# Key and query chunks of a hybrid decoder layer: one 512-column product over a whole bank in place of two of 256 columns

## What is computed

```
u = rms_norm(h, mix_norm_g)
proj = u @ w_in
q, k, v, z, xbc, dt_raw, qm, gate_logits = jnp.split(proj, split_points, axis=-1)
...
s_own = jnp.einsum('bhqd,bhjd->bhqj', q_c, k_own) + bias_tab[:, t5_bucket(dist_own)]
p_own = softmax(where(dist_own >= 0, s_own, -inf))
o = jnp.einsum('bhqj,bhjd->bhqd', p_own, v_own)
```

## Time and profile before

| | |
|---|---|
| time, median of 3 runs | 683.9 us (683.73 to 683.92) |
| span of the profiled execution | 682.1 us |
| TensorE busy | 674.4 us, 99% of the span |
| VectorE busy | 493.9 us, 72% |
| ScalarE busy | 370.9 us, 54% |
| mean granted TensorE clock | 0.998 |

### The profile page before, as it was taken

One profiled execution on the slowest core, in us unless ns is written; L12 is line 12 of the kernel. 1 busy time (PEld: TensorE's weight loads), 2 busy tenths in 40 slices (PEclk: granted clock), 3 DMA queues, 4 the chain that ended last, 5 costly groups with the idle time before them and its releaser, 6 DMA issues.

```text
span 682.1 us, 11413 instructions
## 1 busy us (share of the span) xinstructions
PE 674.4 (99%) x4505; PEld 616.7 (90%) x4505; DVE 493.9 (72%) x618; ACT 370.9 (54%) x461; POOL 10.6 (2%) x21
## 2 busy tenths in 40 slices
PE   9999999999999999999999999999999999999996
PEld 6999999999999989999888888888899999999995
DVE  6886979696866766777754655556688777777796
ACT  6568867767455544555533333443555555555552
POOL 0000000000100100000000000000100000000001
PEclk9999999999999999999999999999999999999999
DMA  9775768569185457545566665565445555555521
GB/s 298 239 255 180 247 206 257 165 217 326 62 260 181 144 165 232 177 144 182 165 213 218 215 191 184 193 227 178 168 136 194 187 185 185 188 187 185 192 88 62
DMA packets 99599, 130.92 MB, mean 192 GB/s; under 512 B 5615, under 2 KB 73708, under 8 KB 98924
## 3 DMA queue, kind: packets, MB, share of 16 engines
q1 hardware_dynamic: 98020, 125.27, 56.5%
q10 hardware_dynamic: 1544, 5.16, 2.4%
HBM read 129.31 MB, written 2.68 MB: 193 GB/s over the span
## 4 chain that ended last, share of the span: by engine, by line
PE 98%; DVE 1%; ACT 0%; issue 0%; POOL 0%; POOLq 0%; DVEq 0%
PE ps L364 30%; PE ps L365 30%; PE ps L366 30%; PE ps L676 1%; PE ps L413 1%; PE ps L419 1%; PE ps L661 1%; PE ps L677 1%; PE ps L696 1%; PE ps L713 1%; PE ps L704 0%; DVE h_nat L1744 0%; PE ps L695 0%; PE ps L715 0%; PE ps L769 0%; PE ps L664 0%
## 5 line engine op out<-in xcount | busy, mean ns | idle before, releaser
L336 DVE TENSOR_TENSOR w_lo<-w_raw,w_hi 128x2048 fp32r<-128x2048 f32 x107 | 244.6, 2287 | 88.1 <-ACT w_hi L332 88.1
L332 ACT ACTIVATE w_hi<-w_raw 128x2048 fp32r<-128x2048 f32 x107 | 204.3, 1911 | 100.0 <-PE ps L366 93.9
L364 PE MATMUL ps<-tok_hi,w_hi 128*128 128x256 f32 x864 | 246.6, 285 | 0.4 <-DVE tok_lo L1305 0.4
L365 PE MATMUL ps<-tok_lo,w_hi 128*128 128x256 f32 x864 | 244.4, 283 | 0.0
L366 PE MATMUL ps<-tok_hi,w_lo 128*128 128x256 f32 x864 | 244.4, 283 | 0.0
L364 PEld LDWEIGHTS ps<-tok_hi,w_hi 128*128 128x128 f32 x864 | 165.7, 192 | 2.0 <-DVE w_lo L1299 0.8
L365 PEld LDWEIGHTS ps<-tok_lo,w_hi 128*128 128x128 f32 x864 | 165.7, 192 | 0.4
L366 PEld LDWEIGHTS ps<-tok_hi,w_lo 128*128 128x128 f32 x864 | 165.7, 192 | 0.0
L364 PE MATMUL ps<-w_hi,tok_hi 128*128 128x512 f32 x128 | 50.2, 392 | 0.0
L365 PE MATMUL ps<-w_lo,tok_hi 128*128 128x512 f32 x128 | 49.9, 390 | 0.0
L366 PE MATMUL ps<-w_hi,tok_lo 128*128 128x512 f32 x128 | 49.8, 389 | 0.0
(11 more groups left out here) (268 smaller groups left out, 1003.5 us busy)
## 6 DMA issues: line engine op xcount, KB each, us to landing
w_raw<-w_in SPq DMA_DIRECT2D x94, 512.0 KB, 4.8
w_raw<-w_ffn_up SPq DMA_DIRECT2D x44, 512.0 KB, 4.4
w_raw<-w_ffn_down SPq DMA_DIRECT2D x22, 512.0 KB, 4.1
w_raw<-w_mem_kv SPq DMA_DIRECT2D x16, 512.0 KB, 4.6
w_raw<-w_br_ssm SPq DMA_DIRECT2D x16, 512.0 KB, 4.9
acs_b<-acs_d ACTq DMA_DIRECT2D x4, 1024.0 KB, 6.6
w_raw<-w_br_attn SPq DMA_DIRECT2D x8, 512.0 KB, 4.9
w_raw<-w_br_mem SPq DMA_DIRECT2D x8, 512.0 KB, 4.5
```

What stands on the lines that cost most here:

```text
L332: act.activation(w_hi[:, s, :], w_raw[:, s, :], ACT.Copy).then_inc(hi_ready[s], 1)
L336: dve.tensor_tensor(w_lo[:, s, :], w_raw[:, s, :], w_hi[:, s, :].bitcast(F32), ALU.subtract).then_inc(lo_ready[s], 1)
L364: pe.matmul(o, a[0], b[0], start=start, stop=False, **kw)
L365: pe.matmul(o, a[0], b[1], start=False, stop=False, **kw)
```

## The change

`tok_hi` and `tok_lo` are laid beside each other, so that the 512 columns of both parts are one moving operand. For the key and query chunks `gemm_both` takes the place of `gemm_cols`: the weights' high part times both token parts in one product of 512 columns over a whole bank, then the weights' low part times the tokens' high part, 256 columns, onto the first half. Each half `j` now has a bank of its own: banks 0 and 1 for keys, 3 and 4 for the queries of pair 0, 6 and 7 for those of the other pairs. The second half of each bank has to be added to the first: ScalarE copies the second halves into `k_t` (a new instruction) or `q_t`, and VectorE adds the first halves (in place of its key copy, and new for the query). Since bank 7 also holds the attention output of pair 0 and of pair 1, the second half of a query chunk waits for `oa_lo_s`. Two semaphores of the memory norm become one, and no transfer is moved.

```diff
+K_BANKS = (0, 1)
...
-    tok_hi = place("tok_hi", 72, [KT, T], F32R)
-    tok_lo = place("tok_lo", 80, [KT, T], F32R)
+    tok = place("tok", 72, [KT, 2, T], F32R)
+    tok_hi, tok_lo = tok[:, :, 0, :], tok[:, :, 1, :]
...
+    def gemm_both(pe, r, s, banks, both, other=None):
+        pe.wait_ge(lo_ready[s], r + 2)
+        pe.wait_ge(bank_free[s], r + 1)
+        for j in range(2):
+            if other is not None and j:
+                pe.wait_ge(*other)
+            for k in range(KT):
+                w = slice(k * CW + j * P, k * CW + (j + 1) * P)
+                pe.matmul(ps[:, banks[j], :], w_hi[:, s, w], both[:, k], start=k == 0, stop=False)
+                mm = pe.matmul(ps[:, banks[j], 0:T], w_lo[:, s, w], both[:, k, 0, :], start=False, stop=k == KT - 1)
+        mm.then_inc(gemm_done[s], 1)
...
+    def q_banks(i):
+        return (6, 7) if i else (3, 4)
+    def part_pair(banks, n):
+        return ps[:, banks[0]:banks[1] + 1, n * T:(n + 1) * T]
...
-            gemm_cols(pe, RB, 0, tok_hi, tok_lo)
-            gemm_cols(pe, RB, 1, tok_hi, tok_lo)
+            pe.wait_ge(xdt_ready, NT * GROUPS)
+            pe.wait_ge(bank_free[1], RB + 1)
+            gemm_both(pe, RB, 0, K_BANKS, tok)
+            gemm_both(pe, RB, 1, q_banks(0), tok)
...
             for i in range(1, 4):
-                gemm_cols(pe, RB + i, 0, tok_hi, tok_lo)
+                if i == 1:
+                    pe.wait_ge(y_step, GT * GROUPS)
+                gemm_both(pe, RB + i, 0, K_BANKS, tok)
                 if i > 1:
                     pe.wait_ge(oa_lo_s, i - 2)
                     pe.wait_ge(group_var, 1)
                     attend(i - 1)
                 turn_probs(i)
-                gemm_cols(pe, RB + i, 1, tok_hi, tok_lo)
+                gemm_both(pe, RB + i, 1, q_banks(i), tok, (oa_lo_s, i - 1))
                 gemm_wide(pe, RB + i, i % 2, tok_hi, tok_lo)
                 if i == 1:
+                    pe.wait_ge(bank_free[1], RB + 3)
                     group_sums()
                 scores(i)
...
+                act.wait_ge(gemm_done[0], r + 1)
+                act.activation(k_t[:], part_pair(K_BANKS, 1), ACT.Copy).then_inc(low_part, 1)
                 split_hi(act, r + 1, 0)
...
                 act.wait_ge(gemm_done[1], r + 1)
-                act.activation(q_t[:], halves(1), ACT.Copy, scale=DH ** -0.5).then_inc(bank_free[1], 1)
+                act.activation(q_t[:], part_pair(q_banks(i), 1), ACT.Copy, scale=DH ** -0.5).then_inc(low_part, 1)
...
-                dve.wait_ge(gemm_done[0], r + 1)
-                dve.tensor_copy(k_t[:], halves(0)).then_inc(bank_free[0], 1)
+                dve.wait_ge(low_part, 2 * i + 1)
+                dve.tensor_tensor(k_t[:], part_pair(K_BANKS, 0), k_t[:], ALU.add).then_inc(bank_free[0], 1)
                 split_lo(dve, r + 1, 0)
...
+                dve.wait_ge(low_part, 2 * i + 2)
+                dve.scalar_tensor_tensor(q_t[:], part_pair(q_banks(i), 0), DH ** -0.5, q_t[:], ALU.mult,
+                                         ALU.add).then_inc(bank_free[1], 1)
                 split_lo(dve, r + 1, 1)
```

More of the change, by code:

```diff
@@ L269, in build @@
         sem, ("group_mm", "group_var", "group_pow", "group_kept", "rstd_g_in"))
+    low_part = sem("low_part")
     s_mm, s_biased, s_max, s_neg, p_exp, p_rec, p_norm, p_turned, pt_ready, o_mm, oa_hi_s, oa_lo_s = map(
@@ L274, in build @@
     norm_step, os_hi_s, os_lo_s = map(sem, ("norm_step", "os_hi_s", "os_lo_s"))
-    m_in, m_sumsq, m_var, m_rstd, m_scaled, mx_in, m_factor_kept, m_factor_in, m_hi, m_lo = map(
-        sem, ("m_in", "m_sumsq", "m_var", "m_rstd", "m_scaled", "mx_in", "m_factor_kept", "m_factor_in", "m_hi", "m_lo"))
+    m_in, m_sumsq, m_var, m_rstd, m_scaled, mx_in, m_factor_moved, m_hi, m_lo = map(
+        sem, ("m_in", "m_sumsq", "m_var", "m_rstd", "m_scaled", "mx_in", "m_factor_moved", "m_hi", "m_lo"))
     ms_mm, ms_max, ms_neg, mp_exp, mp_rec, mp_norm, mp_turned, mo_mm, om_hi_s, om_lo_s = map(
@@ L1105, in _ @@
             act.wait_ge(m_rstd, NT)
-            act.dma_start(m_factor_d.rearrange("(p t) -> p t", p=P), stat[:, 2:2 + NT]).then_inc(m_factor_kept, 16)
+            act.dma_start(m_factor_d.rearrange("(p t) -> p t", p=P), stat[:, 2:2 + NT]).then_inc(m_factor_moved, 16)
             def mem_high(j):
@@ L1112, in _ @@
             squares(GROUPS)
-            act.wait_ge(m_factor_kept, 16)
-            act.dma_start(m_factor[:], on_all(m_factor_d, T)).then_inc(m_factor_in, 16)
+            act.wait_ge(m_factor_moved, 16)
+            act.dma_start(m_factor[:], on_all(m_factor_d, T)).then_inc(m_factor_moved, 16)
             for i in range(1, 4):
@@ L1511, in heads @@
                 if i == 1:
-                    dve.wait_ge(m_factor_in, 16)
+                    dve.wait_ge(m_factor_moved, 32)
                     dve.wait_ge(mx_in, 16)
```

## The result

The changed kernel takes 696.81 us (median of 5 runs, 693.94 to 698.72) against 683.92 us (5 runs, 683.73 to 684.80): 1.0183 times as long, interval 1.017 to 1.0196. It is 12.9 us slower; the forecast was 10.5 us slower.

What follows compares the result with a forecast made beforehand. TensorE's own stream was taken as the bound, since it hardly waits. -1.5 (products) + 6.5 and 3.3 (waits) + 2.2 (clock) = +10.5 us, from 683.9 to 694.4 us; own range 692.4 to 695.8, 8-in-10 range 691.0 to 697.4.

Steps and rivals of the forecast that it cites:

- the second rival: TensorE's clock falls in both `oa_lo` waits: 2.2 us more than the forecast, 696.6 us, chance 0.21.
- products: Key and query chunks: 348 ns a block instead of 360, over 128 blocks, 1.5 us gained; bounds 0 and 2.5.
- wait in pair 2: Pair 2's query chunk: TensorE stands for `oa_lo` from 218.6 to 225.1, 6.5 us; bounds 6.0 and 6.9.
- wait in pair 3: Pair 3's query chunk: TensorE stands for `oa_lo` of the pair 2 scores' softmax, 3.3 us; bounds 2.9 and 3.8.
- other new waits: `xdt_ready`, `y_step`, the query's release by VectorE, pair 0's earlier transposes: price 0, at most 0.2 us.
- clock behind the first wait: TensorE's clock falls to its lower level in pair 2's wait: 2.2 us lost; bounds 0 and 2.7.
- clock behind the second wait: Pair 3's 3.3 us wait: loss from a fall of TensorE's clock taken as 0; bounds 0 to 2.7 us.
- The clock of that working: Times for pair 2's wait, counted from the key chunk's start at 208.07 us; the whole stretch moves earlier by earlier gains.
- The 0.48 us taken for ScalarE's key copy: Pair 2: the new copy delays the high part as the like-shaped query copy delayed its next instruction, 222.41 to 222.89.
- I take 0 for it: Pair 3's 3.3 us wait, barely as long as the idle time before the end's clock fall: no clock loss.
- The change of shape costs nothing there: Feed-forward stage: where a 512 follows a 256 the starts lie 0.12 us apart, 613.65 to 613.77.
- the prediction's own line of 0.35 us a block: Key and query chunks: the prediction is wrong if alternating products step wider than 0.35 us a block.

Runs made afterwards that it cites:

- without waits: Changed kernel with high and low parts of the attention output of pairs 0 and 1 moved earlier, new products kept: 683.05 us, 0.9989 times before.
- first wait filled: Changed kernel with 26 products on zeros put ahead of the wait for `oa_lo` in pair 2's query chunk: 694.32 us, ratio 1.0151.
- the second move alone: Changed kernel with only pair 1's `oa_lo` moved earlier, so the wait in pair 2 stays: 691.53 us, ratio 1.0113.
- both waits filled: Changed kernel with 26 products on zeros in pair 2's wait and 11 more in pair 3's: 692.82 us, ratio 1.0129.
- the first move alone: Changed kernel with only pair 0's `oa_lo` moved earlier, so the short wait in pair 3 stays: 687.87 us, ratio 1.0065.
- the grouped order: Kernel with both `oa_lo` moved, each half chunk's 8 products of 512 columns first, its 8 of 256 behind: 682.62 us, ratio 0.9985.

## Why the prediction was right, and what it mis-sized

The range held the time and the side was right. The forecast's case was that the clock falls in one wait; by the runs it falls in both, which was the second rival (696.6 us, chance 0.21). The range of 691.0 to 697.4 us held the 696.81 because it took that rival in: the forecast's own range ended at 695.8. Nor does that own range follow from its bounds. With 0 to 2.7 us for the clock at each wait they give 691.3 to 698.5. That the rival came within 0.2 us is partly luck, since its two falls were priced 0.4 us too high together and its gain 0.6 us too large. In order of the prediction's terms:

| term | forecast, us | measured, us | from |
|---|---|---|---|
| products | -1.5 | -0.9 | without waits against before, medians |
| wait in pair 2 | +6.5 | +6.4 | waits (6.5 as a step between starts) |
| wait in pair 3 | +3.3 | +3.1 | waits (3.2 as a step) |
| other new waits | 0 | 0 | no row names them |
| clock behind the first wait | +2.2 | +2.5 | change against first wait filled (2.1 by the second move alone) |
| clock behind the second wait | 0 | +1.5 | first against both waits filled (1.7 by the first move alone) |
| sum | +10.5 | +12.6 | 12.9 by the medians |

**The waits.** Place, cause and length were as worked out. The clock of that working ran 0.70 us late as a whole, as it had said it might: the query chunk began at 215.00, not 215.70, and `oa_lo` ended at 224.37, not 225.1. Both moved alike, so their difference stood. The 0.48 us taken for ScalarE's key copy from its like was 0.47.

**The clock.** The step that failed is "I take 0 for it" for the second wait. It rested on one row, the fall some 3 us behind the program's last product, and took a wait of 3.3 us for too close to that to count. In the profiled execution of the change this held, as the clock stayed full behind 3.07 us of standing. Where only this wait was left, and where the first was filled, profiles show it fallen behind 3.07 and 3.12 us. Taking 0 for an event on the edge was the wrong reduction: worked as a coin's toss it would have added about 0.9 us (half of 1.7). The first wait's 2.2 was inside its bounds, 0.3 below the 2.5 that the medians give; the profiled execution itself lost only 1.39 there. The 2.2 was sized by the program's start, where products on zeros ran some 5.5 us at half pace. Behind the waits less was lost in each of the four falls that were profiled, 1.4 to 1.7 us. The start is also a row read by pace alone, as the granted clock in that trace stands at 1.00 from 0 to 8 us. What decides in which execution a wait of 3 us makes the clock fall is open. That the five runs of the change spread over 4.8 us, and those with the first or both waits filled over 0.2, fits a loss behind the first wait that varies with where the wait ends. This is argued from the spread and not shown, since only one execution of each kernel was profiled, and the kernel with the short wait alone spread over 1.6 us too.

**The products.** Both spacings were right for products of one shape, and the term was too large: 0.9 us by the medians and 0.98 by the chunks of the traces, where 1.5 was forecast. "The change of shape costs nothing there" was read off a single change from 256 to 512. In the change, six blocks from 215.43 to 217.56 take 355 ns each, not 348, while six from 243.36 to 245.44 take 347. The wider step crosses the prediction's own line of 0.35 us a block, beyond which it called itself wrong. So the gain differs by chunk: pair 3's key chunk went from 5.93 to 5.84 us and pair 2's from 5.93 to 5.74, where 0.19 was forecast for each. Of the missing 0.5 us the grouped order brings back 0.28; the rest was not tested by itself. The rival that products cost their lengths is excluded: the mean length of the 512-column product is 404 ns in the kernel without waits, and the chunk barely shrinks.

**The rule on idle gaps.** The Trainium skill's "TensorE: Matmul & The Clock Gate", section "Why this matters for your kernels", warns against idle gaps between bursts of products, since the clock falls back to its lower level. The runs agree: a saving of 0.9 us on products opened 9.5 us of gaps and 4.0 us of slow clock behind them.

## What to carry to other kernels

When a product is made to fill a whole bank, ask who last reads that bank: a wait that was no wait while the half was free can cost many times what the wider product saves (13.8 us for 0.9 here). Here it was mended by moving the last reader, not by undoing the product. On an engine that never waits, price a new gap as its length plus the slow clock behind it, 1.5 to 2.5 us here, and don't put that at zero because the gap is only as long as the shortest that is known to cause a fall. If a gap can't be closed, products on zeros in it can bring the second part back, as they did here (4.0 us).

## What the hardware showed that was not expected

- A gap of 3.1 us in TensorE's work cost 1.5 to 1.7 us more behind it, against 2.1 to 2.5 us behind a gap of 6.4 us. Of these two lengths, the double one cost less than double behind itself.
- Filling the gaps took the spread of the runs from 4.8 us (693.94 to 698.72) to 0.2 us (692.71 to 692.92), besides 4.0 us of time. Filling the long one alone already did that for the spread (694.23 to 694.45).
- Products of 512 and 256 columns in turn step by 347 ns a block in some chunks and by 353 to 355 in others. Grouped by shape, the chunk looked at takes 349 ns, and eight chunks take 45.63 us instead of 45.91.
